# Three tiles of the attention's output projection, over seven of eight channel blocks, computed between the parts of the last attention pair

## What is computed

```python
p = jax.nn.softmax(s, axis=-1).astype(v_win.dtype)      # per row of the 16 x 64 grid: 128 window keys + 256 context keys
o = einsum('bhqrc,bhrqcd->bhqd', p_win, v_win) + einsum('bhqk,bkhd->bhqd', p_ctx, v_ctx)
yl = o.transpose(1, 0, 3, 2, 4).reshape(B, S, D) @ w_o
xl = xl + g1 * yl
```

## Time and profile before

| | us |
|---|---|
| median of 3 runs | 3047.37 (3046.45 to 3048.17) |
| span of the profiled execution | 3040.4 |
| TensorE busy | 2898.9 |
| VectorE busy | 1954.0 |
| GpSimd busy | 921.6 |
| ScalarE busy | 866.6 |

### The profile page before, as it was taken

How to read it: one execution, slowest core, us unless ns; L and a number is a source line. 1 busy time by engine, 2 the same in 40 slices (tenths; PEclk the granted TensorE clock), 3 DMA queues, 4 the chain that set the end, 5 groups by cost and what they waited for, 6 DMA issues and landing times.

```text
span 3040.4 us, 45152 instructions
## 1 busy us (share of the span) xinstructions
PE 2898.9 (95%) x15546; PEld 2431.6 (80%) x15546; DVE 1954.0 (64%) x3260; ACT 866.6 (29%) x1537; POOL 921.6 (30%) x615
## 2 busy tenths in 40 slices
PE   4999999999999999999999899999798999999997
PEld 2888887788888888888789788888676878888885
DVE  3776775776667666744551566666614887777777
ACT  3211111411111111111241466666623222222222
POOL 1112111111111111112111344545421456565652
PEclk7999999999999999999999899999999999999998
DMA  7122214022221222111055565555640111111111
GB/s 295 46 66 83 72 55 93 32 65 75 72 78 57 78 77 78 52 42 41 35 154 130 151 177 155 168 151 146 191 144 28 42 42 48 55 48 55 48 55 63
DMA packets 178773, 269.43 MB, mean 89 GB/s; under 512 B 70656, under 2 KB 122880, under 8 KB 178688
## 3 DMA queue, kind: packets, MB, share of 16 engines
q1 hardware_dynamic: 178688, 268.32, 28.8%
HBM read 222.13 MB, written 50.07 MB: 90 GB/s over the span
## 4 chain that ended last, share of the span: by engine, by line
PE 78%; DVE 9%; issue 5%; ACT 3%; DMA 3%; POOL 1%; SPq 1%; DVEq 0%; ACTq 0%; POOLq 0%
PE psum L797 33%; PE psum L835 20%; PE psum L1167 5%; PE psum L1025 5%; PE psum L980 4%; PE psum L1079 2%; PE psum L1048 2%; PE psum L823 2%; PE psum L1062 2%; DVE residual L1724 1%; DVE prod_lo L2086 1%; DMA o_dram<-o_st_lo 1%; PE psum L884 1%; DVE part L2080 1%; PE psum L728 1%
## 5 line engine op out<-in xcount | busy, mean ns | idle before, releaser
L1724 DVE SCALAR_TENSOR_TENSOR residual<-psum,modulation,residual 128x512 f32<-128x512 f32 (+1 forms) x1072 | 715.6, 688 | 584.7 <-PE psum L835 581.4
L2174 POOL TENSOR_TENSOR w_lo<-raw,w_hi 128x1024 fp32r<-128x1024 f32 x158 | 396.6, 2521 | 1484.5 <-ACT w_hi L1217 1481.8
L835 PE MATMUL psum<-prod_hi,w_hi 128*128 128x512 f32 (+1 forms) x1072 | 403.6, 377 | 21.8 <-DVE residual L1724 7.3
L797 PE MATMUL psum<-act_hi,w_hi 128*128 128x512 f32 (+1 forms) x1608 | 405.4, 359 | 6.2 <-POOL w_lo L2192 4.3
L797 PE MATMUL psum<-act_lo,w_hi 128*128 128x512 f32 (+1 forms) x1608 | 405.3, 359 | 0.0
L797 PE MATMUL psum<-act_hi,w_lo 128*128 128x512 f32 (+1 forms) x1608 | 405.0, 358 | 0.0
L835 PE MATMUL psum<-prod_hi,w_lo 128*128 128x512 f32 (+1 forms) x1072 | 395.7, 369 | 0.0
L835 PE MATMUL psum<-prod_lo,w_hi 128*128 128x512 f32 (+1 forms) x1072 | 394.9, 368 | 0.0
L1217 ACT ACTIVATE w_hi<-raw 128x1024 fp32r<-128x1024 f32 x158 | 165.8, 1062 | 712.1 <-PE psum L797 607.3
L797 PEld LDWEIGHTS psum<-act_hi,w_hi 128*128 128x128 f32 x1608 | 284.5, 188 | 61.1 <-issue 4.9
L797 PEld LDWEIGHTS psum<-act_hi,w_lo 128*128 128x128 f32 x1608 | 268.0, 188 | 47.1
(11 more groups left out here) (205 smaller groups left out, 5148.6 us busy)
## 6 DMA issues: line engine op xcount, KB each, us to landing
raw<-ffn_panels SPq DMA_DIRECT2D x132, 512.0 KB, 3.8
mod_in<-mod_rest SPq DMA_DIRECT2D x64, 384.0 KB, 3.1
raw<-conv_panels SPq DMA_DIRECT2D x32, 512.0 KB, 5.3
mod_raw<-mod_panels SPq DMA_DIRECT2D x24, 512.0 KB, 8.2
more_row<-mod_panels SPq DMA_DIRECT2D x48, 256.0 KB, 2.8
k_hi<-k_dram SPq DMA_DIRECT2D x32, 320.0 KB, 5.7
k_lo<-k_dram SPq DMA_DIRECT2D x32, 320.0 KB, 7.3
v_st<-v_dram SPq DMA_DIRECT2D x32, 320.0 KB, 7.1
```

The lines of the kernel that those rows point to most:

```text
L797: mm = pe.matmul(psum[:, bank + b, 0:tn], w[:, s, kb, :], acts[h][:, kb, t0:t0 + tn], start=(kb == 0 and n == 0), stop=(kb == KB - 1 and n ...
L835: mm = pe.matmul(psum[:, 6 + r % 2 if bank is None else bank, 0:tn], w[:, s, ob, :], h[:, t0:t0 + tn], start=(n == 0), stop=(n == 2))
L1724: dve.scalar_tensor_tensor(out=residual[:, ob, t0:t0 + tn], in0=psum[:, 6 + r % 2 if bank is None else bank, 0:tn], scalar=modulation[:, g ...
L2174: pool.tensor_tensor(panel(w_lo, s), raw[:, s], panel(w_hi, s), ALU.subtract).then_inc(lo_done[s], 1)
```

## The change

Three (block, tile) items of the output projection, `WO_EARLY` = (1, 0), (1, 1), (0, 1), are computed over the channels of pairs 0 to 6 in the last pair's `fill`: 21 matmuls each, in chunks of 4, 4, 4, 4 and 5, at steps 6 to 10, 13 to 17 and 20 to 24. They use bank 7, so the last pair's values use bank 6 alone. ScalarE copies each result to `wo_partial` after `pt_high` of groups 12, 19 and 26. In the output stage these items only run over pair 7's channels (`kb` 7), and VectorE adds the kept partial with a step of its own in front of the usual one. The loads of `o` for pairs 3, 4 and 5 move to one place, before the store of pair 6's last unit; that of pair 6 goes behind store 0 of pair 7. The waits on `o` are split over four semaphores.

```diff
         def value_bank(i, u):
-            return PV_BANK + u % 2 if isinstance(i, int) and i == PAIRS - 1 else PV_BANK
+            return PV_BANK
+        WO_EARLY = ((1, 0), (1, 1), (0, 1))
+        O_GROUP = (0, 0, 0, 1, 1, 1, 2, 3)
+        O_FIRST = {0: 96, 3: 96, 6: 32, 7: 32}
+        WO_MATMULS = 3 * (PAIRS - 1)
+        WO_CHUNKS = {first + n: (item, 4 * n, WO_MATMULS if n == 4 else 4 * n + 4)
+                     for item, first in enumerate((6, 13, 20)) for n in range(5)}
+        WO_DRAINED = {12: 0, 19: 1, 26: 2}
...
                 load_v(i, 1)
+                if not heads:
+                    for pair in (3, 4, 5):
+                        load_o(pair)
                 if not first:
                     store_o(i - 1, UNITS - 1)
                 store_o(i, 0)
                 if not heads:
-                    load_o(3)
+                    load_o(6)
...
                 store_o(i, 1)
-                if not heads:
-                    load_o(4)
...
+            def wo_matmuls(item, lo, hi):
+                ob, b = WO_EARLY[item]
+                t0, tn = LAT[b]
+                if lo == 0:
+                    pe.wait_ge(lo_done[ob], base["wo"][ob] + 1)
+                    if item == 0:
+                        pe.wait_ge(qk_lo_done, NQK * PAIRS)
+                    else:
+                        pe.wait_ge(wo_kept, item)
+                for r in range(lo, hi):
+                    kb, part = divmod(r, 3)
+                    if part == 0 and item == 0 and kb in O_FIRST:
+                        pe.wait_ge(o_in[O_GROUP[kb]], O_FIRST[kb])
+                    w, h = ((w_hi, o_hi), (w_hi, o_lo), (w_lo, o_hi))[part]
+                    mm = pe.matmul(psum[:, QK_BANK, 0:tn], w[:, ob, kb, :], h[:, kb, t0:t0 + tn],
+                                   start=(r == 0), stop=(r == WO_MATMULS - 1))
+                if hi == WO_MATMULS:
+                    mm.then_inc(wo_part, 1)
             def fill(i, group, reach):
+                if reach == 0:
+                    if group in WO_CHUNKS:
+                        wo_matmuls(*WO_CHUNKS[group])
+                    return
...
+            def wo_project(p):
+                s = p % 4
+                pe.wait_ge(lo_done[s], base["wo"][s] + p // 4 + 1)
+                for kb in range(KB):
+                    if kb == PAIRS - 1:
+                        pe.wait_ge(o_in[O_GROUP[kb]], O_FIRST[kb])
+                    for n, (w, h) in enumerate(((w_hi, o_hi), (w_hi, o_lo), (w_lo, o_hi))):
+                        for b, (t0, tn) in enumerate(LAT):
+                            early = (p, b) in WO_EARLY
+                            if early and kb < PAIRS - 1:
+                                continue
+                            mm = pe.matmul(psum[:, 6 * (p % 2) + b, 0:tn], w[:, s, kb, :], h[:, kb, t0:t0 + tn],
+                                           start=(n == 0 and kb == (PAIRS - 1 if early else 0)),
+                                           stop=(kb == KB - 1 and n == 2))
+                            if kb == KB - 1 and n == 2:
+                                mm.then_inc(y_ready, 1)
...
+                    if last and group in WO_DRAINED:
+                        item = WO_DRAINED[group]
+                        act.wait_ge(wo_part, item + 1)
+                        act.activation(wo_partial[:, item, :], psum[:, QK_BANK, :], ACT.Copy).then_inc(wo_kept, 1)
...
+                    if (p, b) in WO_EARLY:
+                        item = WO_EARLY.index((p, b))
+                        dve.wait_ge(wo_kept, item + 1)
+                        dve.scalar_tensor_tensor(out=residual[:, p, t0:t0 + tn], in0=wo_partial[:, item, 0:tn],
+                                                 scalar=modulation[:, MODS + 2 * KB + p, 0:1],
+                                                 in1=residual[:, p, t0:t0 + tn], op0=ALU.mult,
+                                                 op1=ALU.add).then_inc(wo_folded, 1)
+                        dve.wait_ge(wo_folded, len(LAT) * p + b)
                     dve.wait_ge(y_ready, len(LAT) * p + b + 1)
```

More of the change, by code:

```diff
@@ L134, in trunk @@
         o_lo, nxt = place("o_lo", [P, PAIRS, TL], F32R, nxt)
+        assert nxt <= weight_at, (nxt, weight_at)
+        wo_partial, nxt = place("wo_partial", [P, 3, BANK], F32, nxt)
         assert nxt <= weight_at, (nxt, weight_at)
@@ L293, in trunk @@
         o_out = sem("o_out")
-        o_most_in, o_last_in = sem("o_most_in"), sem("o_last_in")
+        o_in = [sem(f"o_in{n}") for n in range(4)]
+        wo_part, wo_kept, wo_folded = sem("wo_part"), sem("wo_kept"), sem("wo_folded")
         residual_out = sem("residual_out")
@@ L581, in load_o @@
                 for dst, dram in zip((o_hi, o_lo), o_dram):
-                    sp.dma_start(dst[:, pair].bitcast(F32), dram[pair]).then_inc(o_most_in, 16)
+                    sp.dma_start(dst[:, pair].bitcast(F32), dram[pair]).then_inc(o_in[O_GROUP[pair]], 16)
             load_qk_panel(1, 0)
@@ L627, in attention @@
                 store_o(i, 2)
-                if not heads:
-                    load_o(5)
                 if heads:
@@ L632, in attention @@
                 store_o(i, 3)
-                if not heads:
-                    load_o(6)
                 if heads:
@@ L672, in _ @@
             for dst, dram in zip((o_hi, o_lo), o_dram):
-                sp.dma_start(dst[:, PAIRS - 1].bitcast(F32), dram[PAIRS - 1]).then_inc(o_last_in, 16)
+                sp.dma_start(dst[:, PAIRS - 1].bitcast(F32), dram[PAIRS - 1]).then_inc(o_in[O_GROUP[PAIRS - 1]], 16)
             for kb in range(2, KB):
@@ L1136, in wo_half @@
                 mm.then_inc(norms[3].summed, 1)
[L1138 to L1142, removed]
+            def wo_project(p):
[14 more added lines that the diff above has]
+                                mm.then_inc(y_ready, 1)
+            pe.wait_ge(wo_kept, len(WO_EARLY))
             pe.wait_ge(sum_done, UNITS * PAIRS)
@@ L1145, in _ @@
                 at_least(pe, y_added, len(LAT) * (p - 1))
-                project("wo", p % 4, p // 4, 6 * (p % 2), LAT, y_ready, last_pair, acts=(o_hi, o_lo))
+                wo_project(p)
                 if p == SLOTS:
```

## The result

The changed kernel takes **3055.74 us** (median of 7 runs, 3050.34 to 3058.26) against 3047.37 for the kernel before (7 runs, 3040.0 to 3049.45): ratio 1.0025, 95% interval 1.0015 to 1.0035, which is 4.6 to 10.7 us more. The forecast was 3053.1, with a range of 3047 to 3059. The profiled execution has a span of 3054.3 us in a run of 3056.05.

What follows compares the result with a forecast made beforehand. TensorE, busy 95% of the span, was taken as the bound. The attention's end moves by 8.0 + 4.6 + 0.8 = 13.4 us, the output stage gives back 7.7: net +5.7, 3053.1 us, range 3047 to 3059.

Steps and rivals of the forecast that it cites:

- likeliest case: Whole kernel: later end of the attention outweighs the output stage's gain, net +5.7 us, 3053.1 us; chance 0.50.
- (1): Last pair: the store isn't held up or lands in time, no stall; +0.3 us, 3047.7; chance 0.20.
- (2): Last pair: gaps don't take the matmuls, under 3 of 8.0 us used; net +8.3 us, 3055.7; chance 0.21.
- (3): Last pair: no stall, all 8.0 us of gaps used, slow stretch gone; net -2.9 to -3.9 us; chance 0.06.
- (4): Last pair: a chunk waits for its load of o; 0 to 3 us on top; chance 0.03.
- The matmuls: Last pair: 14.5 us come in, less 5.6 of gaps and 1.7 of slow clock, plus 0.8: 8.0 us later.
- the 1.7: Last pair, 2201.4 to 2205.4: the stretch at 0.57 of the clock runs full with chunks there, saving 1.7 us.
- The stall: Last pair: store held behind three loads, step 8 comes 4.6 us later, plus 0.8 for restarting at 1.2 GHz.
- T: Landing of pair 7's o, from which the output stage is counted; forecast to move 13.4 us later.
- The output stage: From the landing of o(7) to the third block: 4.65 us instead of 12.4, giving back 7.7 us.
- The single bank: Last pair, units 2 to 6: costs nothing because chunks cover the sum; uncovered it would be 0.5 us a unit.
- 7.0 us lie around the span: Whole run: profiled span 3040.4 against median 3047.4; the 7.0 us between were taken as outside the span and unchanged.

Runs made afterwards that it cites:

- pair 6's store first: Kernel before, with pair 6's load of o for pair 0 put behind the store of unit 5 instead of ahead: ratio 0.9984.
- two items: Kernel after, loads behind the store and item (0, 1) back in the output stage: ratio 0.9999; with chunks also moved to the gaps: 0.9993.

## Why the prediction was right, and where it wasn't

**The kind and the size.** The forecast was its likeliest case, +5.7 us; the profile's stretch gives +5.2, the ratio +7.6 with an interval of 4.6 to 10.7 (the medians alone +8.4). Of the rivals, (1), the store isn't held, is refuted by ScalarE's 5.28 us; (2) gives nearly the same time by other means (gaps not taken) and doesn't fit TensorE's rows, where the idle times between the 3.17 us and step 24 sum to 0.9 us (one of 0.22 beside those shown), under the 2 that the prediction set as its sign; (3) has no place where the stall is; (4) shows no wait in the kernel after. That the stall is the transfer order is shown twice, by taking it out of the one kernel (-4.1) and putting it into the other (+5.0).

**The matmuls: 8.0 forecast, 8.07 measured.** The main part with the loads behind the store is 52.22, that of the kernel before 44.15. The pieces of the 8.0 (5.6 of gaps, 1.7 of slow clock saved, 0.8 for copy and bank) aren't each shown, so an agreement to 0.1 us is in part luck. The main parts of the two kernels:

```profile
2166.64:2210.79 44.15, 38.31 (x270) 35.31 (x270) 32.76 (x93) 31.79 (x65) 18.72 (x22) 0.91 0.53 170
2173.97:2226.19 52.22, 50.06 (x333) 45.56 (x333) 33.73 (x93) 32.79 (x68) 18.86 (x22) 0.94 0.42 147
```

By this count 11.8 us of work came in and 3.7 of idle time went, where the forecast had 12.8 (14.5 - 1.7) and 4.8 (5.6 - 0.8), counted by starts: both about 1 us too large. The last unit's wait is shown: 1.12 us at 2227.66, for the forecast 0.8.

The reason given for the 1.7 is not shown. The last 14 us of the main part, before, after, and in the kernel before with the loads ahead:

```profile
2196.79:2210.79 14.00, 11.11 (x74) 9.90 (x72) 9.59 (x24) 9.45 (x20) 4.96 (x6) 0.88 0.43 138
2215.76:2229.76 14.00, 12.18 (x80) 10.34 (x79) 6.48 (x14) 7.88 (x17) 3.32 (x5) 1.00 0.29 94
2199.57:2213.57 14.00, 10.71 (x80) 9.13 (x78) 9.86 (x24) 10.21 (x21) 5.67 (x7) 1.00 0.24 65
```

The slow clock there did go, and 14 x 0.12 is 1.7. But it also went where no matmul had been moved in, only the stall stood earlier. So that the chunks keep the clock up is argued and not shown, and the +4.85 of the loads alone is the stall's price less what this stretch gave back.

**The stall: 4.6 + 0.8 forecast, 3.9 measured** (56.16 - 52.22). ScalarE waited 5.28, not 6.0, and TensorE 3.17, not 3.9. About half of the 1.5 us is the length of the stall, and half a term that failed, the slow clock of 0.8: it rested on idle times of 4.95 and 5.55 us that came back at 1.2 GHz, and 3.17 us came back at full clock. The price was taken from rows of longer waits. Nor does the length of the wait alone decide, as the last section shows; what does stays open.

**T: 13.4 forecast, 12.5 measured** (the landing of `o(7)`, 2241.35 - 2221.84, less the 7.0 that the two executions were apart at step 0). The stall is 1.5 less than forecast, the matmuls 0.1 more, and `o(7)` lands 11.6 us after the end of the main part for 11.1 before, 0.5 that no term had.

**The output stage: 7.7 forecast, 7.4 measured.** From T to the third block 4.87 (forecast 4.65) instead of 12.36 is 7.5; over the rest of the blocks 0.1 of it is lost again. The wait is 5.98 for 5.5, at 1.2 GHz behind it as forecast (0.69 of full clock over the 4.87 us). VectorE's row shows the fold:

```profile
2243.97 0.75 DVE L2086 SCALAR_TENSOR_TENSOR residual<-psum,modulation,residual 128x512 f32<-128x512 f32 x1 [13.74 <-PE psum L1181]
2244.64 0.74 DVE L2080 SCALAR_TENSOR_TENSOR residual<-wo_partial,modulation,residual 128x512 f32<-128x512 f32 x1
2245.41 0.75 DVE L2086 SCALAR_TENSOR_TENSOR residual<-psum,modulation,residual 128x512 f32<-128x512 f32 x1
```

The fold takes 0.74 us, as long as the step that reads PSUM (0.75), at the upper end of the bounds of 0.4 to 0.75; to the start of the step behind it, which waits for it, are 0.77, against 0.67 from the first step to the fold. The third block started 0.8 us after the last of these three steps began, so VectorE's chain decides there and TensorE's 0.45 us of idle time is the price.

**The single bank** was given as free in units 2 to 6 under cover, and that stands: 2.1 us without cover, and waits of 0.22 to 0.36 us with it.

**"7.0 us lie around the span"** was wrong. A run and the span of its profile differ by 1.75 to 1.87 us in every kernel here (3056.05 and 3054.3). The rest of the 7.0 is spread between executions: the profiled one was among the shorter ones. The forecast wasn't hurt, since a difference was added to a median.

**Interleaving, and the order on a queue.** Moving the matmuls paid only where they met idle time: 42 matmuls cost 4.9 or 3.1 us by their place, and a bank had to be given up for them. The Trainium skill, Perfetto Trace Analysis, Optimization Strategy, says that interleaving regimes with different most-contended engines may improve performance; these runs agree for some places and not for others. A store behind 3 MB of loads took 9.2 us, and one ahead of them 2.3. The Trainium skill, DMA: Bandwidth & Descriptors, Queues, rings and completion order, says that each DMA engine consumes descriptors in ring order, and the runs agree. It also says that completion isn't first-in first-out per issuing engine; this didn't show here as a store that overtook.

## What to carry to other kernels

When work is moved into gaps, list every transfer that has to be moved for it and ask what small, urgent store or load now stands behind it in the queue: here three megabytes ahead of 64 KB cost four times what the moved matmuls cost net. The best place for moved matmuls was in front of a long wait (7.1 us for 28 matmuls before 5.8 us of wait, 2.0 before 1.74 us), then the steps that have gaps, and last a fixed pattern of steps. That long wait was made by the change itself, which had taken the third item away from in front of it. And compare two profiles from a common instruction right ahead of the change: with unchanged code, that instruction alone lay up to 12.6 us apart between executions.

## What the runs showed of the hardware

- TensorE after idle time in the last pairs: behind 1.57 us (pair 6's store first) and 3.17 us (after) four transposes take 0.66, full clock; behind 3.73 us (matmuls left out) 0.83 and a granted clock of 0.57 over the next 4 us; behind 4.49 us (loads ahead) 1.12 and 0.50. At the wait for pair 7's `o`, 1.74 and 2.26 us of idle time (two items) were followed by full clock, 5.80 and 5.98 by 1.2 GHz. But the length of the idle time alone doesn't decide: in front of unit 5's first scores in pair 6 TensorE stood 2.32 us in the kernel before and 2.27 in the kernel after, with the same code up to there, and over the next 3 us the granted clock was 1.00 in the one and 0.50 in the other. The stall with 3.17 us cost the main part 3.9 us, the one with 4.49 us 4.85.
- A 64 KB store on SP's queue took 2.3 us from issue to landing with the loads of pair 7 behind it, 9.2 with three megabytes of them ahead, and 5.8 when it was issued 3.0 us after the last of them; in pair 6 it took 10.1 us with `load_o(0)` ahead and 6.1 without. Where loads were ahead it landed 0.4 us after the last of them (kernel after: 2186.0 and 2186.4) and 0.3 us after (loads ahead in the kernel before: 2177.1 and 2177.4).
- ScalarE's copy of a full bank took 0.59 us, the same as the `stage_hi` copies of the earlier trace rows, with another output type. VectorE's `scalar_tensor_tensor` over 512 columns takes 0.75 us with its first operand in PSUM and 0.74 with it in SBUF.
